# Row norms at nine places: sums of squares in four column groups, the root and reciprocal on a quarter of the columns

## The reference, cut to what matters

```python
def rms_norm(x, gain):
    xf = x.astype(jnp.float32)
    y = xf * lax.rsqrt(jnp.mean(xf * xf, axis=-1, keepdims=True) + EPS)
    return (y * gain.astype(jnp.float32)).astype(x.dtype)

# first block                                  D_MODEL = 1024, 512 tokens
h = modulate(rms_norm(x, norm1_g), ...)        # norm1
h2 = modulate(rms_norm(x, norm2_g), ...)       # norm2, ahead of the experts
return rms_norm(x, final_g)                    # final
# second block, two layers                     512 tokens of x, 256 of ctx
hx, hc = rms_norm_2(x, g_pre), rms_norm_2(ctx, g_pre)          # pre 0, pre 1
q = rms_norm_2(q_lat, g_qa) @ w_qb             # qn, over 384 features
kv = rms_norm_2(kv_lat, g_kva) @ w_kvb         # kvn, over 256 features
x = x + gate_x * rms_norm_2(out_x, g_post)     # post 0 (with ctx), post 1 (x alone)
```

## Time and profile before

| | us |
|---|---|
| median of 3 runs (lowest, highest) | 3867.21 (3866.64, 3868.18) |
| the profiled execution | 3873.01 |
| its span, first to last instruction | 3871.1 |
| TensorE matmul busy | 3620.1 (94%) |
| VectorE busy | 2161.4 (56%) |
| ScalarE busy | 1414.5 (37%) |

### The profile page before, as it was taken

One profiled execution on the slowest core, in us unless ns is written; L12 is line 12 of the kernel. 1 busy time (PEld: TensorE's weight loads), 2 busy tenths in 40 slices (PEclk: granted clock), 3 DMA queues, 4 the chain that ended last, 5 costly groups with the idle time before them and its releaser, 6 DMA issues.

```text
span 3871.1 us, 53964 instructions
## 1 busy us (share of the span) xinstructions
PE 3620.1 (94%) x21015; PEld 3063.3 (79%) x21015; DVE 2161.4 (56%) x4547; ACT 1414.5 (37%) x2285; POOL 762.4 (20%) x645
## 2 busy tenths in 40 slices
PE   6999998989998997999997899999999879999997
PEld 4877886878898997999995458868888745687885
DVE  3353343498989657787884454275333254537443
ACT  3232323323444442333334453263112335526222
POOL 0000000006988873465530000000000000000000
PEclk8999999999999998999998999999999989999998
DMA  5223223467887889999992001101111211120232
GB/s 212 98 77 142 98 95 118 148 208 272 281 282 264 309 287 360 359 354 323 375 352 86 22 28 55 60 18 46 65 66 66 76 55 39 61 82 23 98 103 82
DMA packets 220555, 594.49 MB, mean 154 GB/s; under 512 B 17936, under 2 KB 101520, under 8 KB 215952
## 3 DMA queue, kind: packets, MB, share of 16 engines
q1 hardware_dynamic: 156592, 380.68, 28.8%
q0 software_dynamic: 36864, 134.23, 9.7%
q10 hardware_dynamic: 26848, 76.14, 5.2%
HBM read 530.16 MB, written 60.82 MB: 153 GB/s over the span
## 4 chain that ended last, share of the span: by engine, by line
PE 77%; DVE 11%; DMA 7%; issue 2%; ACT 2%; POOL 0%; ACTq 0%; DVEq 0%; SPq 0%
PE bank L742 60%; PE bank L941 7%; DMA WR<-in_vrows 3%; PE bank L1035 2%; PE bank L1021 2%; PE bank L908 2%; DVE WL L1509 2%; PE bank L766 1%; DMA gelu_by_expert<-geU 1%; PE bank L803 1%; DMA rows<-in_urows,rk 1%; DMA rows<-in_vrows,rk 1%; DMA WR<-in_weights 1%; DVE Rw L1770 1%; ACT WH L1126 0%
## 5 line engine op out<-in xcount | busy, mean ns | idle before, releaser
L1509 DVE TENSOR_TENSOR WL<-WR,WH 128x1024 fp32r<-128x1024 f32 x512 | 627.7, 1228 | 823.4 <-ACT WH L1126 764.9
L1126 ACT ACTIVATE WH<-WR 128x1024 fp32r<-128x1024 f32 x512 | 537.1, 1058 | 811.3 <-DMA WR<-in_weights 201.2
L742 PE MATMUL bank<-H2h,WH 128*128 128x512 f32 (+2 forms) x1624 | 578.5, 356 | 4.5 <-DVE H2l L1537 4.5
L742 PE MATMUL bank<-H2h,WL 128*128 128x512 f32 (+2 forms) x1624 | 573.4, 353 | 0.0
L742 PE MATMUL bank<-H2l,WH 128*128 128x512 f32 (+2 forms) x1624 | 572.9, 353 | 0.0
L742 PE MATMUL bank<-Hh,WH 128*128 128x384 f32 (+1 forms) x1440 | 526.8, 366 | 25.7 <-DVE WL L1509 25.6
L742 PE MATMUL bank<-Hh,WL 128*128 128x384 f32 (+1 forms) x1440 | 511.9, 355 | 0.0
L742 PE MATMUL bank<-Hl,WH 128*128 128x384 f32 (+1 forms) x1440 | 511.2, 355 | 0.0
L941 PE MATMUL bank<-ah,WH 128*128 128x384 f32 x1024 | 346.0, 338 | 31.2 <-issue 18.0
L673 POOL DMA_INDIRECT rows<-in_urows,rk x128 | 164.9, 1288 | 960.4 <-DVE rk L1795 740.9
L742 PEld LDWEIGHTS bank<-H2h,WH 128*128 128x128 f32 (+1 forms) x1624 | 307.1, 189 | 52.3 <-issue 7.7
(11 more groups left out here) (310 smaller groups left out, 5679.4 us busy)
## 6 DMA issues: line engine op xcount, KB each, us to landing
WR<-in_weights SPq DMA_DIRECT2D x498, 512.0 KB, 3.5
WR<-in_vrows SPq DMA_DIRECT2D x128, 512.0 KB, 9.4
gelu_by_expert<-geU ACTq DMA_DIRECT2D x128, 192.0 KB, 4.8
gates_by_expert<-tab ACTq DMA_DIRECT2D x24, 1024.0 KB, 6.3
geV<-gelu_by_expert SPq DMA_DIRECT2D x32, 768.0 KB, 12.0
Gt<-gates_by_expert SPq DMA_DIRECT2D x16, 1536.0 KB, 18.4
x_kept<-X ACTq DMA_DIRECT2D x2, 3072.0 KB, 8.7
X<-x_kept ACTq DMA_DIRECT2D x2, 3072.0 KB, 11.0
```

The source lines that it names most:

```text
L742: yield nc.tensor.matmul(b[0:rows, out_cols], a, r, start=n == 0, stop=n == len(pairs) - 1)
L1126: act.activation(WH[:, n % SLOTS, :, :].rearrange("p a b -> p (a b)"), WR[:, c % SLOTS, :, :].rearrange("p a b -> p (a b)"), ACT.Copy)\
L1509: v.tensor_tensor(WL[:, n % SLOTS, :, :].rearrange("p a b -> p (a b)"), WR[:, plan.splits[n] % SLOTS, :, :].rearrange("p a b -> p (a b)"), ...
```

## The change

The sums of squares are cut into four groups of columns. Group g is summed with 32 columns of ones into the partitions 32g to 32g+31 of one bank, so that a bank of 128 partitions by a quarter of the columns (q = 128 or 192) holds all of them. Root and reciprocal work on that quarter. Then four products spread group after group back to all partitions: 32 rows of ones by the same 32 rows of `rt`, each into a bank of its own. ScalarE copies the first two out of PSUM, VectorE the last two. Each product sums 32 equal rows, so the root is scaled by 32 (with `epsq` for the epsilon). The two jobs of a norm over 768 columns become one, and four jobs are added to each norm.

The order changes in four places. kvn goes ahead of qn, and TensorE waits for the scaled kv tiles alone ahead of `vb`. The spread of norm1 stands one modulation product later than its sums, and the eight scalings with it. Behind norm2, ScalarE's two copies stand ahead of the load of `sub`. At the start, the six loads of constants stand ahead of the load of x in ScalarE's queue.

```diff
+SPREAD = (1, 2, 3, 0)
@@ make_plan
+    def spreads(key):
+        for g in SPREAD:
+            p.job((*key, "to", g), "V" if g in SPREAD[2:] else "A")
         if f == NORM1_AT:
-            p.job(("norm1", "x"), "A")
+            p.job(("norm1",), "A")
+        if f == NORM1_AT + 1:
+            spreads(("norm1",))
@@ TensorE
-            def sum_squares(keys_cols, src, n):
-                for i, (key, cols) in enumerate(keys_cols):
-                    w = cols.stop - cols.start
-                    product(key, slice(0, w), [(ones[:, :], src(j)[:, cols] if callable(src) else src[:, j, cols])
-                                               for j in range(n)], tiles=None if i else sq_ready)
+            def sum_squares(key, src, n, w):
+                q = w // QUADS
+                def calls(b):
+                    for j in range(n):
+                        pe.wait_ge(sq_ready, k.next(sq_ready))
+                        for g in range(QUADS):
+                            yield nc.tensor.matmul(b[QUAD * g:QUAD * (g + 1), 0:q], ones[:, 0:QUAD],
+                                                   src(j)[:, g * q:(g + 1) * q], start=j == 0, stop=j == n - 1)
+                fill(key, calls)
+
+            def spread_norm(key, r_, w):
+                pe.wait_ge(norm_ready, k.next(norm_ready))
+                for g in SPREAD:
+                    p0 = slice(QUAD * g, QUAD * (g + 1))
+                    product((*key, "to", g), slice(0, w // QUADS), [(ones[p0, :], r_[p0, 0:w // QUADS])])
...
-                sum_squares([(("qn", l, c), xcols(c)) for c in xc], lambda j: lat_sq(j), QL)
-                sum_squares([(("kvn", l, c), xcols(c)) for c in ("x", "c")], lambda j: lat_sq(QL + j), KVL)
-                pe.wait_ge(lat_ready, k.next(lat_ready, QL + KVL))
+                sum_squares(("kvn", l), lambda j: lat_sq(QL + j), KVL, A)
+                sum_squares(("qn", l), lambda j: lat_sq(j), QL, A if upd else T)
+                spread_norm(("kvn", l), rk, A)
+                spread_norm(("qn", l), rt, A if upd else T)
+                pe.wait_ge(lat_ready, k.next(lat_ready, KVL))
@@ ScalarE
             dma(vec[:, :], d["vec"][:, :]).then_inc(vec_loaded, 16)
-            dma(XT[:, :, :], d["x"][:, :, :]).then_inc(x_loaded, 16)
             at = 0
             for name, w in CONSTS:
                 dma(consts[name][:, :], d["consts"][:, at:at + w]).then_inc(small_loaded, 16)
                 at += w
+            dma(XT[:, :, :], d["x"][:, :, :]).then_inc(x_loaded, 16)
...
+            def root(key, r_, w, n):
+                out_of(key, r_[:, 0:w // QUADS], slice(0, w // QUADS), ACT.Sqrt,
+                       scale=QUAD * QUAD / n, bias=epsq[:, 0:1])
+            def spread_norm(key, r_, w):
+                q = w // QUADS
+                for g in SPREAD[:2]:
+                    out_of((*key, "to", g), r_[:, g * q:(g + 1) * q], slice(0, q))
...
-            root(("norm2", "x"), rt[:, 0:T], slice(0, T), D)
+            root(("norm2",), rt, T, D)
+            spread_norm(("norm2",), rt, T)
             dma(tab[:, 0:2048], d["sub"][:, :]).then_inc(sub_loaded, 16)
@@ VectorE
+            def inverted(key, r_, w):
+                dve.wait_ge(act_read, act_at(key))
+                v.reciprocal(r_[:, 0:w // QUADS], r_[:, 0:w // QUADS]).then_inc(norm_ready, k.inc(norm_ready))
+            def spread_norm(key, r_, w):
+                q = w // QUADS
+                for g in SPREAD[2:]:
+                    v.tensor_copy(r_[:, g * q:(g + 1) * q], bank_of((*key, "to", g))[:, 0:q])\
+                        .then_inc(dve_read, k.inc(dve_read))
+                dve.wait_ge(*k.own())
+                dve.wait_ge(act_read, act_at((*key, "to", SPREAD[1])))
...
-                v.reciprocal(rt[:, 0:w], rt[:, 0:w]).then_inc(dve_step, k.inc(dve_step))
...
-                v.reciprocal(rk[:, :], rk[:, :]).then_inc(dve_step, k.inc(dve_step))
...
+                inverted(("kvn", l), rk, A)
+                inverted(("qn", l), rt, w)
+                spread_norm(("kvn", l), rk, A)
+                for j in range(KVL):
+                    v1(LAT[:, QL + j, :], LAT[:, QL + j, :], V(f"kva{l}", j), rk[:, :], ALU.mult, ALU.mult)\
+                        .then_inc(lat_ready, k.inc(lat_ready))
+                spread_norm(("qn", l), rt, w)
```

More of the change, by code:

```diff
@@ L222, in make_plan @@
     lin("w_out", ("w_out", 0), "V", 8)
-    p.job(("norm2", "x"), "A")
+    p.job(("norm2",), "A")
+    spreads(("norm2",))
     for f in range(17):
@@ L249, in make_plan @@
         p.job(("V", dd), "V")
-    p.job(("final", "x"), "A")
+    p.job(("final",), "A")
+    spreads(("final",))
     for l in range(LAYERS):
@@ L253, in make_plan @@
         xc = ("x", "c") if upd else ("x",)
-        p.job(("pre", l, "x"), "A")
-        p.job(("pre", l, "c"), "A")
+        p.job(("pre", l), "A")
+        spreads(("pre", l))
         def queries_a():
@@ L334, in queries_b @@
             p.job(("krbp", l), "V")
[L335 to L338, removed]
+            p.job(("kvn", l), "A")
+            p.job(("qn", l), "A")
+            spreads(("kvn", l))
+            spreads(("qn", l))
             p.chunk(("vb", l), ("vb", l), False)
@@ L355, in make_plan @@
         lin(("wo", l), ("w_o", l), "A", 8, xc)
-        for c in xc:
-            p.job(("post", l, c), "A")
+        p.job(("post", l), "A")
+        spreads(("post", l))
     p.row_of = {n: i for i, n in enumerate(n for n, what in enumerate(p.chunks) if what[0] != "V")}
@@ L947, in _ @@
                     .then_inc(filled, 1)
-            sum_squares([(("final", "x"), slice(0, T))], XF, KD)
+            norm(("final",), XF, T)
             for l in range(LAYERS):
@@ L953, in _ @@
                 xc = ("x", "c") if upd else ("x",)
-                sum_squares([(("pre", l, c), xcols(c)) for c in ("x", "c")], X2W, KD)
+                norm(("pre", l), X2W, A)
                 def queries_a():
@@ L1101, in _ @@
                                tiles=t_split if f == 0 and c == "x" else None)
-                sum_squares([(("post", l, c), xcols(c)) for c in xc], OS, KD)
+                norm(("post", l), OS, A if upd else T)
         @block.scalar
@@ L1352, in _ @@
                 dma(x_dram[:, :, :], X2[:, :, :]).then_inc(x_kept, 16)
-                for c in ("x", "c"):
-                    root(("pre", l, c), rt[:, xcols(c)], slice(0, T if c == "x" else C), D)
+                root(("pre", l), rt, A, D)
+                spread_norm(("pre", l), rt, A)
                 shift(X2W, H2h, lambda c, j: pre[:, l, 0 if c == "x" else 1, j:j + 1],
@@ L1489, in _ @@
                         dma(X2[:, :, :], x_dram[:, :, :]).then_inc(x_back, 16)
-                for c in xc:
-                    root(("post", l, c), rt[:, xcols(c)], slice(0, T if c == "x" else C), D)
+                root(("post", l), rt, w, D)
+                spread_norm(("post", l), rt, w)
             act.wait_ge(res_ready, k.next(res_ready, KD))
@@ L1935, in _ @@
                 w = A if upd else T
[L1936 removed]
+                normed(("pre", l), X2, X2W, H2h, H2l, A)
                 def queries_a():
@@ L2138, in _ @@
                     low_tile(H2l[:, f, 0:w], M4[:, f, 0:w], H2h[:, f, 0:w])
-                for c in xc:
-                    dve.wait_ge(act_read, act_at(("post", l, c)))
-                v.reciprocal(rt[:, 0:w], rt[:, 0:w]).then_inc(dve_step, k.inc(dve_step))
-                dve.wait_ge(*k.own())
+                inverted(("post", l), rt, w)
+                spread_norm(("post", l), rt, w)
                 dve.wait_ge(x_back, k.at(x_back, 16 * (l + 1)))
```

73 lines of the change are left out of this document (36 added, 37 removed).

## The result

| | before | after |
|---|---|---|
| median of the runs, us | 3867.69 (3866.64 to 3877.19, 4) | 3805.42 (3802.31 to 3807.41, 4) |
| ratio, 95% interval | | 0.983 (0.9818 to 0.9843) |
| profiled execution, us (span) | 3873.0 (3871.1) | 3802.31 (3800.3) |
| mean granted clock | 0.970 | 0.968 |

The changed kernel takes 62.3 us less by the medians and 70.8 by the spans of the two profiled executions. The median of before now has a fourth run in it (3877.19) beside the three of the first table. The forecast was 3806 with 61.4 saved.

The account below looks back on a forecast made before the run. TensorE held 77% of the chain, but whole norms on VectorE, with long reciprocals, left it idle. Terms summed to 61.4 us off 3873.0, so 3811.6; with the median 5.8 lower, 3806 (range 3797 to 3815, chance 0.66).

Parts of the forecast that it names:

- the eight places: norm2, final, pre 0, latents 0, post 0, pre 1, latents 1, post 1: a microsecond off the norm shortens the kernel equally.
- Rival D: Most norm places: something else was late anyway, so the time stays within 7 us of before; chance 0.04.
- rival C: More gain: spreads overlap (0.45, 0.7 us), clock holds at norms, start gives 9 us; 3793 us in all; chance 0.08.
- final and pre 0: The final norm and the next layer's first norm: shorter norms save 3.7 and 8.7 us.
- post 0 and pre 1: Norms where layer 0 ends and layer 1 begins: shorter norms save 9.65 and 6.5 us.
- norm2: Norm ahead of `together`: the load of sub becomes the late one, so 2.7 us are saved, not 5.5.
- the latents: Latent norms of layers 0 and 1: values start sooner, saving 10.5 and 7.8 us, plus 1 each for the clock.
- post 1: Last norm of layer 1: counted from the end of the table load, it saves 5.65 us.
- the start: Kernel start with norm1: earlier squares 3, shorter sums 4.9, less 3.0 waiting and 0.7 clock; saves 4.2 us.
- The term for the clock: Value products behind both latent norms: shorter idle time may keep the clock up; 1 us counted at each, 2 in all.
- Rival E: Dense TensorE stretches behind each norm stay at the low clock, making the kernel slower, 3886 us; chance 0.03.
- The rule on tiling modes: Each norm's three mode changes drain TensorE: at most 0.2 us a norm, eleven norms, 2 us, giving 3808.

## Why the prediction was right, and where it was off

**The frame held.** Reciprocals of 3.4 and 5.0 us stood in the chain as links of their own, and shortening them shortened the kernel at every one of the eight places. The experiments show both halves at work: reciprocals back, +39.3 us; sums back, +46.2. Rival D (within 7 us of before) falls with that.

**Prices.** Root and reciprocal were as fitted. A tile's sum was taken at 0.29 and 0.43 us; it is 0.25 and 0.35 in a row of tiles, and 0.53 for a lone tile of 192 columns, which is what stands behind the last square. The spread was taken at 0.8 and 1.2 us; it is 0.50 and 0.61 at full clock, near rival C's 0.45 and 0.7, and 0.81 and 1.02 at half. The 0.8 and 1.2 were thus nearly the half-clock prices, while I added more for a low clock besides. The terms fell short by 4.5 us (61.4 against 65.9): final and pre 0 by 1.2 and post 0 and pre 1 by 0.9, which this price explains against the profile of before that the forecast used (with the other one, post 0 and pre 1 saved 15.5 us, less than the 16.15 forecast); norm2 by 0.4, half of it by a load of sub that landed in 6.3 us and not 6.5; the latents and post 1 by 0.4 in all; and the start by 1.5, which is not this price.

**The start.** 4.2 against 5.7. I let x land at 16.4, since "the bytes of the queue are the same"; it landed at 15.5. The move gave 4.0 us by itself and not 3, and the quarters 1.7 and not 1.2. The sums took 2.99 us where I had 4.6. Against that, the granted clock stood at half from 27.62 to 54.93 us, where before it stood there from 44.34 to 61.40 (ahead of 24 and 31 us there are no clock records, but the matmuls have their half-clock durations, 0.42 us against 0.27 for 128 columns of a group), so nearly all modulation products behind the norm ran at the low level (1.01 to 1.08 us for 16 records, against 0.57); the 0.7 us that I took off for it were not measured by themselves, since the waits for weights lie over them. My working of the wait in TensorE's order was right in sign: with full sums in the new order the start takes 55.66 us, no less than before, though the constants are ahead.

**norm2.** Right: the load of sub became the late one and the gain was 3.1, not 5.5; moving it gave the missing 2.6.

**Latents.** 12.2 and 8.3 against 11.5 and 8.8. From the last square to the values it is 5.5 and 5.1 us, where I had 6.0 and 5.6 and before had 16.5 and 13.4: the path was right. The reordering is worth 3.1 and 2.1 us. The term for the clock (1 us at each) was wrong: TensorE's few products in the gap did not keep it up, and the values began at half clock as before. Those of layer 0 took 12.03, 12.60 and 12.64 us in three profiles against 12.41, those of layer 1 12.66, 12.23 and 12.30 against 13.34, or 12.45 in the profile with the constants alone.

**The clock.** Rival E fell: it wanted some 120 to 160 us more at the low level, and the clock records have 236 us of it before and 240, 223 and 229 us in three profiles of the changed kernel. In the 30.7 us from 3041.6 the granted clock stood at 0.5, the 1.2 GHz level, through post 0's scaling, pre 1 and the first 4.5 us of the dense work; before, it rose twice in between and was at half again until 4.0 us behind the start of that work, so the change cost 0.3 us in the dense work (half of 0.6). The two layers took 2.1 and 1.6 us longer in the first pair (0.4 and 0.6 in the two later profiles against the first of before); short stretches of the low clock lie in them (3.4 us at 3509 and at 3731 in after), and their cause was not tested. The profile with the constants alone, whose layers are those of before, took 917.32 and 650.65 us, so layer 1 varies by 2.6 us without any change in it.

**The number.** 3806 against 3805.42 is closer than the working deserves. The terms were 4.5 us short. Against it, the layers took 1 to 4 us longer, which may be chance as well, and I took the median to lie 5.8 us below the profiled execution, where the chance of the long stretch lies. Three groups of runs give 62.3, 65.1 and 64.0 us saved, against 61.4 forecast.

**The rule on tiling modes.** The spread of 128 columns takes 0.50 us, of which a second round repeats 0.25: what is left for filling, handing on and any change of mode at the spread is 0.25 us, in eleven norms under 3 us. The changes at the sums were not measured. The Trainium skill, page "TensorEngine Tiling (Array Packing)", section "Tiling Modes", says that a change of mode drains TensorE; no run here separates that from the rest of the 0.25. By the time alone 3808, with that rule, and 3806 can't be told apart, since the runs of one kernel differ by more.

**Table loads.** From the last square of final to the root the profile shows 1.31 us, 1.28 of them the load. The Trainium skill, page "ScalarE: Activation LUTs", section "Table sets: the hidden batching unit", puts a load at about 2.7 us; its section "What ACT_TABLE_LOAD costs" makes that up of 1283 ns for the load and 1380 ns for a drain. The trace agrees with the load alone: the root starts 0.01 us behind it, no drain shows, and 1.28 decides. To have the load out of the way, which the page's advice to batch by set comes to here, was worth 0 to 0.65 us at the norms behind the start, since the sums covered the rest.

## What to carry to other kernels

A value that is equal on all partitions need not be computed on all columns: split the columns over the partitions with column groups, do the slow elementwise work on a quarter, and spread it back by row groups, for 0.5 to 1.0 us of TensorE and 1.2 to 1.8 us with the copies. Before you count a wait as cover, look at what stands ahead of its issue on the same queue. And judge single edits of 2 to 5 us by cutting the traces at the same instructions; medians of five runs could not tell them from nothing.

## What was not expected of the hardware

- Four products of 32 rows by 128 columns, in four row groups, take 0.50 us at full clock and 0.25 more for a second round; for 192 columns 0.61 and 0.35.
- Sums in four column groups, 32 products of 192 columns, run in 2.81 us, 0.35 a tile; a lone tile takes 0.53 at full and 0.87 at the low clock.
- A table load took 1.28 us wherever it stood, and a root could start 0.01 us behind it; a root of one column ahead of eight squares caused no second load.
- A stretch of 1430 us with the same instructions varies by 12 us from one execution to the next, which is more than most edits of this study bring.
